# A two-layer encoder trunk on one core: the layer norm seams taken by token halves, normalisation on ScalarE, GpSimd held at the seam

## The reference, cut to what matters

```python
h = layer_norm(ALPHA * h + 0.5 * swiglu(h, wg, wu, wd), g[0], b[0])     # q = 0
h = layer_norm(ALPHA * h + hybrid_mixer(h, ...), g[1], b[1])            # q = 1
h = layer_norm(ALPHA * h + 0.5 * swiglu(h, wg2, wu2, wd2), g[2], b[2])  # q = 2
h = layer_norm(ALPHA * h + sigmoid(h @ ple_gate) * (p @ ple_proj), g[3], b[3])  # q = 3
```

## Time and profile before

| | |
|---|---|
| median of three runs | 3225.05 us |
| the profiled execution, its own time | 3221.0 us |
| its span, first to last instruction | 3219.2 us |
| TensorE busy | 3045.5 us, 95% of the span |
| GpSimd busy | 2104.3 us, 65% |
| VectorE busy | 1589.3 us, 49% |
| ScalarE busy | 566.0 us, 18% |
| mean granted TensorE clock | 0.976 of full speed |

### The profile page before, as it was taken

One profiled execution on the slowest core, in us unless ns is written; L12 is line 12 of the kernel. 1 busy time (PEld: TensorE's weight loads), 2 busy tenths in 40 slices (PEclk: granted clock), 3 DMA queues, 4 the chain that ended last, 5 costly groups with the idle time before them and its releaser, 6 DMA issues. The chain is left out here.

```text
span 3219.2 us, 45211 instructions
## 1 busy us (share of the span) xinstructions
PE 3045.5 (95%) x19506; PEld 2502.9 (78%) x19506; DVE 1589.3 (49%) x1811; ACT 566.0 (18%) x915; POOL 2104.3 (65%) x941
## 2 busy tenths in 40 slices
PE   8999999889999999999899999998899999999996
PEld 6888787777777878888688887777777778788875
DVE  5321334766656683221882215248666486722127
ACT  1000025443310010000110000353433100100000
POOL 7888675322238878887788877753221578788874
PEclk9999999999999999999899999999999999999998
DMA  4333332111113333323223323311210123333231
GB/s 139 98 96 96 98 118 60 42 49 31 31 40 97 119 97 104 97 94 98 92 92 98 98 93 104 105 55 35 55 40 22 60 88 122 104 99 93 97 105 66
DMA packets 202019, 267.75 MB, mean 83 GB/s; under 512 B 12352, under 2 KB 130460, under 8 KB 201692
## 3 DMA queue, kind: packets, MB, share of 16 engines
q1 hardware_dynamic: 195200, 244.82, 25.1%
q10 hardware_dynamic: 6620, 20.04, 1.8%
HBM read 258.52 MB, written 6.29 MB: 82 GB/s over the span
## 5 line engine op out<-in xcount | busy, mean ns | idle before, releaser
L1081 POOL TENSOR_TENSOR w_hi<-w_raw,zero 128x1024 fp32r<-128x1024 f32 (+2 forms) x468 | 945.7, 2021 | 1040.1 <-PE ps L838 1029.5
L1084 POOL TENSOR_TENSOR w_lo<-w_raw,w_hi 128x1024 fp32r<-128x1024 f32 (+2 forms) x468 | 1160.7, 2480 | 36.8
L838 PE MATMUL ps<-hT_hi,w_hi 128*128 128x512 f32 x2288 | 917.0, 401 | 18.2 <-DVE hT_lo L1536 10.1
L838 PE MATMUL ps<-hT_lo,w_hi 128*128 128x512 f32 x2288 | 897.0, 392 | 0.0
L838 PE MATMUL ps<-hT_hi,w_lo 128*128 128x512 f32 x2288 | 896.7, 392 | 0.0
L838 PEld LDWEIGHTS ps<-hT_hi,w_hi 128*128 128x128 f32 x2288 | 431.7, 189 | 118.5 <-issue 16.5
L838 PEld LDWEIGHTS ps<-hT_hi,w_lo 128*128 128x128 f32 x2288 | 431.8, 189 | 92.7
L838 PEld LDWEIGHTS ps<-hT_lo,w_hi 128*128 128x128 f32 x2288 | 432.5, 189 | 89.0 <-issue 2.9
L1579 DVE TENSOR_TENSOR act_raw<-silu,ps 128x512 f32<-128x512 f32 x88 | 59.8, 680 | 555.7 <-PE ps L838 555.7
L838 PE MATMUL ps<-w_hi,aT_hi 128*128 128x512 f32 x704 | 274.2, 390 | 0.0
L838 PE MATMUL ps<-w_lo,aT_hi 128*128 128x512 f32 x704 | 273.9, 389 | 0.0
(11 more groups left out here) (297 smaller groups left out, 3667.3 us busy)
## 6 DMA issues: line engine op xcount, KB each, us to landing
w_raw<-in_w_in SPq DMA_DIRECT2D x104, 512.0 KB, 3.6
w_raw<-in_ffn_wg SPq DMA_DIRECT2D x176, 256.0 KB, 2.8
w_raw<-in_ffn_wu SPq DMA_DIRECT2D x176, 256.0 KB, 3.1
w_raw<-in_ffn_wd SPq DMA_DIRECT2D x88, 512.0 KB, 3.6
w_raw<-in_w_in SPq DMA_DIRECT2D x96, 128.0 KB, 2.3
w_raw<-in_w_out SPq DMA_DIRECT2D x16, 512.0 KB, 3.7
w_raw<-in_ple_gate SPq DMA_DIRECT2D x16, 512.0 KB, 3.6
ln_rows<-in_ln_g ACTq DMA_DIRECT2D x8, 512.0 KB, 3.9
```

Of the source, the lines that this page charges most:

```text
L838: ins = nc.tensor.matmul(o, l_, r_, start=first, stop=last)
L1081: nc.gpsimd.tensor_tensor(w_split[0][:, q, :, 0:w], w_raw[:, r, :, 0:w], zero[:, 0:1].unsqueeze(2).to_broadcast([P, 2, w]), ALU.add).then_ ...
L1084: nc.gpsimd.tensor_tensor(w_split[1][:, q, :, 0:w], w_raw[:, r, :, 0:w], w_split[0][:, q, :, 0:w].bitcast(F32), ALU.subtract).then_inc(*st ...
```

## The change

At a seam the normalised rows now come from ScalarE: VectorE computes `ln_shift` = -mean times reciprocal deviation (128 x 1), and ScalarE writes the 1024 columns as scale times row plus shift (`normalised`). The transposes of tokens 0 to 255 (`first_half`, 16 transposes, two feature blocks to a bank, 4 banks) are placed inside the last product block of the group before; at q = 3 they follow "pproj". The first group of the next step (`dense_from_halves`) makes feature blocks 0 to 3 for tokens 0 to 255 and for tokens 256 to 511 apart (`block(half, k)`; in a feature-major group with 256 columns a matmul), with the other 16 transposes between them into 4 more banks, and feature blocks 4 to 7 over all tokens as before. Of blocks 0 to 3 ScalarE writes `h_raw` and the rounded high part, both out of PSUM, and VectorE subtracts (`low_part`, 256 columns). Of blocks 4 to 7 VectorE itself scales and shifts out of PSUM (`features`), and then rounds and subtracts over 512 columns. GpSimd splits slot 1 of such a group by its two rows, and starts on slot 2 only after `low_part` of half 0, block 3. An unused tensor of 8 columns goes, `ln_shift` comes.

```diff
+        halves = [slice(0, 256), slice(256, SEQ)]
+
+        def seam_into(name):
+
+            if name[0] == "up" and name[3] == 0:
+                L, f = name[1], name[2]
+                return (L, 1) if f else (L - 1, 3) if L else None
+            return {"sb": (name[1], 0), "pgate": (name[1], 2)}.get(name[0]) if name[-1] == 0 else None
...
-            def dense(name, x, feature_major, freed, own_x=None, among=every, tail=0):
-
-
+            def open_group(name, x, feature_major, freed, among):
...
-                out_b = []
+                out_b = {}
                 n0 = at_slot[0]
-
-                def products(i, kk, m):
+                into = seam_into(name)
+                def products(i, kk, m, half=None):
                     r, k, ins = (n0 + i) % SPLIT_RING, 2 * i + kk, None
-                    if k == 0:
-                        out_b.append(take((*name, m), freed(m), among))
+                    if k == 0 and m not in out_b:
+                        out_b[m] = take((*name, m), freed(m), among)
...
+                        first = k == 0 and (xp, wp) == (0, 0) and not (feature_major and half == 1)
...
+                        if aside is not None and (m, i) == (n_tiles - 1, n_slots - 1):
+                            aside()
...
+            def transposes(L, q, half, ks, ts):
+
+                for k in ks:
+                    if k % 2 == 0 and ts[0] % 2 == 0:
+                        take(("hT", L, q, half, k // 2), ("hT_raw" if k < 4 else "hT_x", L, q, half, k + 1))
+                    b = ps[banks_of[("hT", L, q, half, k // 2)]]
+                    for t in ts:
+                        c = 256 * (k % 2) + P * (t % 2)
+                        ins = nc.tensor.transpose(b[:, c:c + P], h_tok[:, t, k * P:(k + 1) * P], ident())
+                    if k % 2 and ts[-1] % 2:
+                        ins.then_inc(*step("hT_done", L, q, half, k // 2))
+
+            def first_half(L, q):
+
+                for t in range(2):
+                    pe.wait_ge(*after("xn_ready", L, q, t))
+                transposes(L, q, 0, range(KD), (0, 1))
+
+            def dense_from_halves(name, feature_major, freed, L, q):
+
+
+
+                products, n0, n_slots, n_tiles = open_group(name, hT, feature_major, freed, every)
+
+                def block(half, k):
+                    pe.wait_ge(*after("w_rest_ready", n0 + k // 2))
+                    pe.wait_ge(*after("hT_half", L, q, half, k))
+                    for m in range(n_tiles) if feature_major else (2 * half, 2 * half + 1):
+                        products(k // 2, k % 2, m, half)
+
+                block(0, 0)
+                block(0, 1)
+                pe.wait_ge(*after("xn_ready", L, q, 2))
+                transposes(L, q, 1, range(4), (2,))
+                block(0, 2)
+                pe.wait_ge(*after("xn_ready", L, q, 3))
+                transposes(L, q, 1, range(4), (3,))
+                block(0, 3)
+                transposes(L, q, 1, range(4, KD), (2, 3))
+                for k in range(4):
+                    block(1, k)
+                for i in range(2, n_slots):
+                    pe.wait_ge(*after("w_rest_ready", n0 + i))
+                    for kk in range(2):
+                        pe.wait_ge(*after("hT_rest", L, q, 2 * i + kk))
+                        for m in range(n_tiles):
+                            products(i, kk, m)
...
-                if q < 0:
-                    parts = [(range(0, 4), range(NT)), (range(4, 8), range(NT))]
-                else:
-                    parts = [(range(0, 4), range(NT - 1)), (range(4, 8), range(NT - 1)), (range(8), [NT - 1])]
...
+                    freed = lambda m: ("silu_done", L, f, g, m) if m < 2 else ("act_raw", L, f, g, m - 2)
+                    if g == 0 and q[1] >= 0:
+                        dense_from_halves(("up", L, f, g), True, freed, *q)
+                    else:
+                        run(dense(("up", L, f, g), hT, True, freed, own_x=stream_split(*q) if g == 0 else None))
...
+                              own_x=arrived if half == 0 else None, tail=2 * half,
+                              aside=lambda: first_half(L, 2 * f)))
...
-                to_feature_major(L, 0)
-
-                for n in range(3):
-                    run(dense(("sb", L, n), hT, n < 2, lambda m: ("sb_in", L, n, m),
-                              own_x=stream_split(L, 0) if n == 0 else None))
+                dense_from_halves(("sb", L, 0), True, lambda m: ("sb_in", L, 0, m), L, 0)
+                for n in range(1, 3):
+                    run(dense(("sb", L, n), hT, n < 2, lambda m: ("sb_in", L, n, m)))
...
+                    if half == 0:
+                        dense_from_halves(("pgate", L, 0), False, lambda m: ("ple_sig", L, 0, m), L, 2)
+                        for k in range(2):
+                            pe.wait_ge(*after("pT_rest", L, k))
+                    else:
+                        run(dense(("pgate", L, half), hT, False, lambda m: ("ple_sig", L, half, m)))
...
-                    to_feature_major(L, 3)
+                    first_half(L, 3)
...
+                into = seam_into(g[0])
+                if into is not None and i == 2:
+
+                    pool.wait_ge(*after("hT_half", *into, 0, 3))
+                for rows in ((slice(0, 1), slice(1, 2)) if into is not None and i == 1 else (slice(0, 2),)):
+                    n_rows = rows.stop - rows.start
+                    nc.gpsimd.tensor_tensor(w_split[0][:, q, rows, 0:w], w_raw[:, r, rows, 0:w],
+                                            zero[:, 0:1].unsqueeze(2).to_broadcast([P, n_rows, w]), ALU.add).then_inc(
+                        *step("w_high", n, rows.stop))
+                    pool.wait_ge(*after("w_high", n, rows.stop))
+                    ins = nc.gpsimd.tensor_tensor(w_split[1][:, q, rows, 0:w], w_raw[:, r, rows, 0:w],
+                                                  w_split[0][:, q, rows, 0:w].bitcast(F32), ALU.subtract)
+                ins.then_inc(*step("w_rest_ready", n))
...
+            def features(L, q, half, k):
+
+                now("hT_done", L, q, half, k // 2)
+                b = ps[banks_of.get(("hT", L, q, half, k // 2), 0)][:, 256 * (k % 2):256 * (k % 2) + 256]
+                g = parT[:, R_LNG + 8 * q + k:R_LNG + 8 * q + k + 1]
+                o = parT[:, R_LNB + 8 * q + k:R_LNB + 8 * q + k + 1]
+                nc.scalar.activation(h_raw[:, k, halves[half]], b, ACT.Identity, bias=o, scale=g)
+                nc.scalar.activation(hT[0][:, k, halves[half]], b, ACT.Identity, bias=o, scale=g).then_inc(
+                    *step("hT_raw", L, q, half, k))
+
+            def deviation_of(L, q, t):
+                now("ln_var", L, q, t)
+                nc.scalar.activation(ln_rstd[:, t, :], ln_mv[:, t, 1:2], ACT.Sqrt, bias=ln_eps[:, :]).then_inc(*step("ln_sqrt", L, q, t))
+
+            def normalised(L, q, t):
+                now("ln_shift", L, q, t)
+                nc.scalar.activation(h_tok[:, t, :], h_tok[:, t, :], ACT.Identity, bias=ln_shift[:, t, :],
+                                     scale=ln_rstd[:, t, :]).then_inc(*step("xn_ready", L, q, t))
...
+                for t in range(2):
+                    deviation_of(L, q, t)
+                    normalised(L, q, t)
+                deviation_of(L, q, 2)
+                if not last:
+                    features(L, q, 0, 0)
+                    features(L, q, 0, 1)
+                normalised(L, q, 2)
+                if not last:
+                    features(L, q, 0, 2)
+                deviation_of(L, q, 3)
+                normalised(L, q, 3)
+                if not last:
+                    features(L, q, 0, 3)
+                    for k in range(4):
+                        features(L, q, 1, k)
...
+            def low_part(L, q, half, k):
+
+                now("hT_raw", L, q, half, k)
+                cols = halves[half]
+                v.tensor_tensor(hT[1][:, k, cols], h_raw[:, k, cols], hT[0][:, k, cols].bitcast(F32), ALU.subtract).then_inc(
+                    *step("hT_half", L, q, half, k))
...
+                for k in range(4, KD):
+                    now("hT_done", L, q, half, k // 2)
+                    b = ps[banks_of.get(("hT", L, q, half, k // 2), 0)][:, 256 * (k % 2):256 * (k % 2) + 256]
+                    v.tensor_scalar(h_raw[:, k, halves[half]], b, parT[:, R_LNG + 8 * q + k:R_LNG + 8 * q + k + 1],
+                                    parT[:, R_LNB + 8 * q + k:R_LNB + 8 * q + k + 1], ALU.mult, ALU.add).then_inc(
+                        *step("hT_x", L, q, half, k))
+
+                features(L, q, 0)
+                low_part(L, q, 0, 3)
+                low_part(L, q, 1, 0)
+                low_part(L, q, 1, 1)
+                features(L, q, 1)
+                low_part(L, q, 1, 2)
+                low_part(L, q, 1, 3)
+                for k in range(4, KD):
...
+                onward = (L, q) != (DEPTH - 1, 3)
+                if t == 3 and onward:
```

(19 more changed lines are left out.)

73 lines of the change are left out of this document (26 added, 47 removed).

## The result

The changed kernel takes 3305.45 us (median of four runs, 3303.17 to 3309.83) against 3225.00 for the kernel before, measured beside it: ratio 1.0252, 95% interval 1.0235 to 1.027, so 80 us slower. The prediction was 3309.0. The profiled execution took 3303.17, its span is 3301.4, 82.2 more than before; its mean granted clock is 0.973, before 0.976.

A forecast was written before the change was run, and what follows sets the result against it. TensorE, busy 95% of the span, was taken as the bound, losing time in seam waits and slow clock. Three "up" seams (43.5), two "sb" (40.5), "pgate" and end 0 made +84: 3305 profiled, 3309 median; range 3268 to 3338.

The forecast's parts named there:

- Blocks of half 0 and 1: First group behind the "up" seam of layer 1: TensorE waits 0.6, 2.1 and 0.9 us; half 1 runs 2765.1 to 2770.7.
- The ladder: Blocks 5 to 7: every rounding waits for a `w_hi`, every subtraction for a `w_lo`; 5.0 us a block, TensorE needs 2.7.
- The bank wait: Second group takes banks of the group just finished and waits: 43.5 us at three "up" seams, 40.5 at two "sb".
- "up" at q = 1: Seam into "up": second group waits for `act_raw` until 2799.0, then a cold start; 14.5 us lost at each of three seams.
- "sb": Two seams into "sb": second group waits for ScalarE's eviction behind `h_scaled`; 19.4 us in layer 0, 21.1 in layer 1.
- The seam at q = 3: Seam into "up" following "pproj", priced like the other "up" seams: 14.5 us lost.
- "pgate" and the end: Two "pgate" seams: no bank wait, between -0.8 and +2, taken 0; kernel's end: shorter VectorE chain, later `ln_rows` issue, 0.
- The rule on the lock: VectorE and GpSimd: a blocked instruction costs its whole length after release; scaling 1.2 us longer a seam, +6 in the sum.
- Rival 1: GpSimd stays out of VectorE's way in splits and scaling, which end early: about -22 us, 3203; chance 5%.
- Rivals 2 to 4: Second groups' bank wait short, 3260 to 3280, 13%; turns last in scaling, up to 3353, 7%; no net change, 3225, 3%.

The follow-up runs named there:

- the two repairs: Changed kernel with the bank order put back and the rounding of blocks 4 to 7 moved from VectorE to ScalarE: 3205.36 us, ratio 0.9938.
- the same edit: Rounding of blocks 4 to 7 moved from VectorE to ScalarE: in the changed kernel 3286.11 us, with the bank order also put back 3205.36 us.
- that run: Changed kernel, banks as they are, with the rounding of blocks 4 to 7 moved from VectorE to ScalarE: 3286.11 us, ratio 1.0186.

## Why the prediction was right, step by step

- **Blocks of half 0 and 1.** Predicted waits of 0.6, 2.1 and 0.9 us; the trace has 0.43, 1.59 and 0.73. Half 1 was to start at 2765.1 and started at 2765.16 on the prediction's clock. The half-width matmul, taken at 0.117, costs 0.12 from start to start.
- **The ladder.** 5.0 us a block predicted, 4.8 measured (2843.09 to 2847.90); block 7 ready at 2783.5, measured 2783.35; the two waits of 2.3 us that it makes for TensorE were 1.88 and 1.75. Its cause as given holds in this kernel: it is not the pause that makes it (without the pause it stayed, at 2.1 and 2.75 us a block). On the kernel before, the pause alone does make it. In the changed kernel the pause is worth 15 us. The prediction counted what it costs, one turn of `low_part` (1, 0) and a hidden delay of slot 2, and not what it saves.
- **The bank wait.** Shown from both sides: putting the order back takes 65 us away, putting it into the kernel before adds 72. The prediction's 43.5 for three "up" seams and 40.5 for two "sb" seams stand against 36.9 and 28.1 for the banks alone. The whole 84 stood in the sum on this wait and the clock behind it, and 65 hang on it. By the sum nothing would be left without it; 15.5 us were.
- **The terms' sizes.** "up" at q = 1 was 12.75 and not 14.5. The second group went on at 2798.55 where 2799.0 was foreseen; what followed, the short wait for m = 3 and the slow clock, was 2.0 us and not 3.1: behind the five long waits 9, 6, 12, 11 and 6 starts were 0.4 us or more apart, not 14. In this seam the clock was down already in the group (starts 0.43 us apart from 2854.35 to 2857.76), so that TensorE came to the bank 1.6 us late, hidden in the wait. "sb" was 18.4 for 19.4 and 19.1 for 21.1, with the eviction 2.65 us behind the last scaling instruction (426.80 to 429.45), not 4.0.
- **The seam at q = 3.** Taken at 14.5 like the other "up" seams, with "pgate" at 0; together they measured 19.2. Of the 6.5 us more than the 12.75 of q = 1, rows give 4.5. Before, the products of this seam have no slow stretch (one start of 0.31 us behind the first, the others 0.23), so there are no 2.8 us to save; its transposes are slow instead, 24 in 5.49 us, as 16 are in 3.65 after. After, the slow stretch behind the bank wait is 1.1 us longer than at q = 1 (12 starts for 6), and 0.6 is the wait for the rows at the next seam. The rest is open; the first half's transposes, which no last group covers here, wait 7.9 us for the rows of both their tiles. This is argued from the rows; no run parts "pgate" from "up" there.
- **"pgate" and the end.** 0 predicted, 0.0 measured for layer 1. It is a balance, not an absence: with the rounding on ScalarE, and so without the ladder, the same stretch was 4.6 us shorter.
- **The rule on the lock.** In the Trainium skill (SBUF — State Buffer, section "Who interferes with whom") the blocked instruction waits for the whole of the other. The scaling instruction of 2857.61 ended 1.09 us after GpSimd's `w_hi` did (2859.32), against 1.22 alone: as in the kernel before, some of a blocked instruction's time has passed when the other ends. The trace differs from the rule by 0.13 us an instruction. The rule was not needed: without its 6 us the sum is 2 us above what was measured.
- **The rivals.** Rival 1 asked for a GpSimd that stays out of the way. Its time, 3203, is near what the two repairs gave (3205.4), by coincidence, since the mechanism was another: GpSimd keeps its turns in the scaling, but no bank hangs on them. Rivals 2 to 4 are out with the five waits at their full length.

The mechanism was right, and the waits stand where it put them. The closeness of the sum was in part luck: its terms miss by 1 to 5 us with both signs, and the errors cancel to 2.

## What to carry to other kernels

When a change moves instructions that take buffers from a pool by age, write out who holds each buffer for the next two groups, and what the release stands behind in its engine's queue. A reorder can cost more through that than through any work it adds, and a few lines of order give it back. Time won ahead of such a wait shows as a longer wait; repair the wait first, then judge the rest (the same edit was worth 21 us with it and 37 without). When you hold an engine back, ask where its next instructions will fall, not just the one held: of three such holds here one cost 38 us, and two were worth 15 and 9.

## What the runs showed of the hardware that I had not expected

- **Turns are not always strict.** Four subtractions in a row on VectorE, their inputs all there, took 2.49 us together, as if alone, while GpSimd's `w_hi`, issued 0.67 us after the first of them, took 3.57 us instead of 1.89. It is so at all five "up" and "sb" seams of that run and of the run with both repairs. So "first asker first" does not hold: by the trace GpSimd asked before the third and the fourth. In the ladder every rounding and every subtraction was held up. There only the subtraction waits by a semaphore for the rounding ahead of it; the next rounding waits for nothing of the kind, and GpSimd got in ahead of it all the same. What a run of like instructions has that keeps GpSimd out is not settled here.
- **A tiny instruction takes a turn too.** The 128 x 1 `ln_shift` took 2.10 us behind a GpSimd instruction, and 0.16 alone; so work moved off VectorE to avoid the turns has to be moved whole, or the rest must be kept out of GpSimd's way.
- **The same short waits come with a lower clock and without.** In the seam laid out, two idle stretches of 1.88 and 1.75 us, 4.7 us apart, were followed by eight starts 0.43 us apart, the lower of TensorE's two levels. The same pair, within 0.04 us, stands at the four other "up" and "sb" seams of the changed kernel, and in layer 0, at q = 0 of the run with the bank order put back (1.85 and 1.74), without a slow stretch ahead of the bank wait. In the kernel before the clock is down from the first product on the earlier trace rows, behind 2.65 and 2.17 us; with a wait of 0.47 and one of 2.94 (normalisation on ScalarE) it fell 1.3 us later, and with 0.98 and 1.34 (the pause alone) it stayed up. What tells these apart was not tried.
